# One step later for the attention's sums and the norm's turns in a fused two-block model kernel

## The reference, cut to what matters

```python
def stick_breaking_mixer(xn, k_sh, v_sh, w_q, w_out):
    ...
        z = jnp.einsum('bhqd,bhnsd->bhqns', qi, kb).astype(jnp.float32)
        log_keep = jnp.where(mask, jax.nn.log_sigmoid(-z), 0.0)
        cs_in = jnp.einsum('bhqnj,js->bhqns', log_keep, tri)
        blk = cs_in[..., 0]
        after = lax.cumsum(blk, axis=3, reverse=True) - blk
        a = jnp.where(mask, jnp.exp(z + cs_in + after[..., None]), 0.0)
        outs.append(jnp.einsum('bhqns,bhnsd->bhqd', a.astype(vb.dtype), vb))

def peer_ffn(xn, w_q, subkeys, u, v):
    ...
    def block(args):
        xc, ec, gc = args
        hid = jnp.einsum('cd,ced->ce', xc, jnp.take(u, ec, axis=0)).astype(jnp.float32)
        w = (gc * jax.nn.gelu(hid, approximate=False)).astype(xc.dtype)
        return jnp.einsum('ce,ced->cd', w, jnp.take(v, ec, axis=0))
```

## Time and profile before

| | |
|---|---|
| median of three runs | 2362.85 us (2358.72 to 2370.2) |
| the profiled execution | 2362.11 us, its span in the trace 2360.3 us |
| PE busy | 1934.7 us (82%) |
| DVE busy | 1629.4 us (69%) |
| ACT, POOL busy | 800.8 us, 661.1 us |
| DMA | 746.58 MB, mean 316 GB/s |
| mean granted TensorE clock | 0.905 of full |

### The profile page before, as it was taken

How to read it: one execution, slowest core, us unless ns; L and a number is a source line. 1 busy time by engine, 2 the same in 40 slices (tenths; PEclk the granted TensorE clock), 3 DMA queues, 4 the chain that set the end, 5 groups by cost and what they waited for, 6 DMA issues and landing times. The chain is left out here.

```text
span 2360.3 us, 32786 instructions
## 1 busy us (share of the span) xinstructions
PE 1934.7 (82%) x12376; PEld 1260.4 (53%) x12376; DVE 1629.4 (69%) x3789; ACT 800.8 (34%) x1826; POOL 661.1 (28%) x657
## 2 busy tenths in 40 slices
PE   3999996688686679889869888885878884999798
PEld 3887886665242136546526555651434432767664
DVE  5668876477978677655667798767798544368853
ACT  3112222133342342454343366344323224233222
POOL 2222110044354433343332335434334430000000
PEclk9999998899797789989989999997898996899899
DMA  8998773179999999999999989999899995222200
GB/s 332 370 363 314 258 262 113 40 323 418 369 409 421 421 408 418 419 414 419 409 412 360 409 304 419 419 411 412 334 419 417 419 419 204 94 81 81 98 11 27
DMA packets 124686, 746.58 MB, mean 316 GB/s; under 512 B 13536, under 2 KB 16608, under 8 KB 56304
## 3 DMA queue, kind: packets, MB, share of 16 engines
q0 software_dynamic: 93792, 610.66, 64.2%
q1 hardware_dynamic: 30736, 133.82, 14.7%
HBM read 741.02 MB, written 3.41 MB: 315 GB/s over the span
## 5 line engine op out<-in xcount | busy, mean ns | idle before, releaser
L1947 DVE CUSTOM_DVE_ANT_0 got<-got,xk 128x1024 f32<-128x1024 f32 x512 | 620.5, 1224 | 318.2 <-DMA got<-in_peer_uv,idx 301.5
L1850 POOL DMA_INDIRECT got<-in_peer_uv,idx x512 | 586.1, 1145 | 906.7 <-PE ps L1812 817.0
L1812 PE MATMUL ps<-got,diag 64*64 64x512 f32 x3936 | 580.6, 684 | 191.2 <-ACT diag L1907 137.6
L1902 ACT ACTIVATE gelu<-eye,hid 128x64 f32<-128x64 f32 x492 | 170.5, 347 | 791.8 <-DVE hid L1947 784.5
L1812 PEld LDWEIGHTS ps<-got,diag 64*64 64x64 f32 x3936 | 121.4, 144 | 441.6 <-ACT diag L1907 274.7
L1342 PE MATMUL ps<-xT,ring 128*128 128x256 f32 x928 | 233.4, 399 | 0.0
L1342 PEld LDWEIGHTS ps<-xT,ring 128*128 128x128 f32 x928 | 174.4, 197 | 77.2 <-issue 55.1
L1028 PE MATMUL ps<-xT,ring 128*128 128x256 f32 x768 | 187.6, 393 | 6.1 <-ACT xT L1143 3.8
L1907 ACT ACTIVATE diag<-gelu,gate 128x64 f32<-128x64 f32 x492 | 171.1, 348 | 46.1 <-ACT gelu L1902 1.1
L1028 PEld LDWEIGHTS ps<-xT,ring 128*128 128x128 f32 x768 | 142.2, 193 | 82.3 <-issue 56.2
L192 POOL DMA_DIRECT2D vring<-in_vslabs x136 | 72.3, 532 | 273.4 <-DVE in_b_psums L304 136.9
(11 more groups left out here) (618 smaller groups left out, 2462.5 us busy)
## 6 DMA issues: line engine op xcount, KB each, us to landing
ring<-in_small SPq DMA_DIRECT2D x158, 512.0 KB
vring<-in_vslabs POOLq DMA_DIRECT2D x136, 512.0 KB, 6.9
ring<-in_slabs SPq DMA_DIRECT2D x18, 2048.0 KB, 10.7
got<-in_peer_uv,idx POOLq DMA_INDIRECT x512
h<-in_x SPq DMA_DIRECT2D x2, 2048.0 KB, 7.9
w_out<-in_slabs SPq DMA_DIRECT2D x2, 2048.0 KB, 9.9
out<-h SPq DMA_DIRECT2D x4, 512.0 KB, 2.6
bias_rows<-brow POOLq DMA_DIRECT2D x1, 1280.0 KB, 4.7
```

The source lines that it names most:

```text
L1812: mm = nc.tensor.matmul(ps[to:to + HALF, i, :], diag[own, d % NDIAG, :], got[own, n % GRING, 1, 512 * g:512 * g + 512], start=(k == 0), st ...
L1850: nc.gpsimd.indirect_dma_start(out=got[:, n % GRING].rearrange("p a d -> p (a d)"), out_offset=None, in_=table, in_offset=bass.IndirectOff ...
L1902: nc.scalar.activation(gelu_of[:, n % 2, :], eye2[:], ACT.Gelu, scale=hid[:, w % 2, k:k + 1]).then_inc(gelu_done, 1)
L1947: nc.vector.tensor_tensor_reduce(row_in, row_in, xk[:, w % 2, :], 1.0, 0.0, ALU.mult, ALU.add, hid[:, w % 2, k:k + 1]).then_inc(dotted, 1)
```

## The change

For pass 1 alone, two numbers of the side plan go up by one. The first step of the turns is 5 instead of 4, so the turns and all that follows them stand one step later, while mean, root and scaling keep steps 2 and 3; the plan has 149 steps instead of 148. And "sums" stands at 5 instead of 4 from its head's first step, so its two parts come at 5 and 6, while "top" stays at 4 and "total" at 7. No instruction is added or removed on any engine; buffers, banks and the arithmetic stay as they are. Since `side_pace` works from the plan, its costs and the slot of each step follow.

```diff
@@ side_plan @@
         each, pitch = (1 if p else 2), 6
         asks = [(0, -4, -2)] if p else [(0, -7, -5), (1, -4, -2)]
-        stages = {"product": 0, "take": 2, "soft": 2, "top": 4, "sums": 4, "total": 7, "expo": 8, "output": 9, "return": 11}
+        stages = {"product": 0, "take": 2, "soft": 2, "top": 4, "sums": 5 if p else 4, "total": 7, "expo": 8, "output": 9, "return": 11}
         at = {"mean": 2, "root": 2, "scale": 3}
-        jobs, s = [], 4
+        jobs, s = [], 5 if p else 4
         jobs += [(s + j // 2, "turn", j) for j in range(4)]
```

## The result

The kernel after takes 2370.56 us, median of 18 runs (2366.2 to 2378.97); the kernel before took 2363.22 beside it (18 runs, 2357.34 to 2370.2). The ratio of the times is 1.003, with a 95% interval of 1.002 to 1.0041: slower, by 7.3 us in the medians. The forecast was 2364.5 in a range of 2354 to 2373, and "within 0.5%" at 0.87. The sign and the class hold, the median is in the range; the size is three times the 2.4 us forecast.

A forecast was written before the change was run, and what follows sets the result against it. Pass 1 was taken as bound by DMA transfers save 15 us of idle. DVE 1.2 us late at slot 345 plus 2.4 made 3.6, less 1.2 in hand: +2.4 on 2362.11 gave 2364.5 us, range 2354 to 2373.

The forecast's parts named there:

- Where the steps go, and PE's order: Planner's slots for each step; in heads 3 to 6, 2.9 us of PE work comes between the sums' two parts.
- The norm's turns: Norm and queries: PE's 0.41 us wait filled, a dot product falls behind DVE's wait; DVE enters the attention 0.8 us later.
- Heads 0 to 2: Slots 298 to 313: PE's 13.9 us of waits go, DVE gains 1.6 us, transfers 3 to 5 us ahead at slot 324.
- Head 3: Attention: "total", which waited 2.80 us, costs 2.1 us more; DMA waits of the next dot products hide 1.5.
- Head 4: Attention: "total", which did not wait before, now waits for the sums' second part, +2.3 us.
- Heads 5 and 6: Attention: "total" waits about 1.5 us each, softplus waits of 3.7 us with head 7 go; these nearly cancel.
- Head 7 and its queue: End of attention: last exponential 1.2 + 2.4 = 3.6 us later, 1.2 us in hand, so the DMA is 2.4 us later.
- That lead is spent: The DMA lead from heads 0 to 2 is used up in the ring of 8 buffers, whatever its size.
- (1): Attention: waits shorter or last output's queue covered, DMA stays 3 to 5 us ahead; 2357 to 2359 us, chance 0.31.
- (2): Attention: nothing that counts changes, ring fills as before, DVE sets the pace; 2361 to 2363 us, chance 0.11.
- (3): Heads 3 on: softplus starts as much later as "total" ends, so its waits stay; +11.3 us, 2373 us, chance 0.13.
- The other sign of being wrong: Profile after: a granted clock differing by more than 0.02, which the forecast had not counted.

The follow-up runs named there:

- after again: The kernel after, unchanged, run once more for a second profile; 2364.38 us, slots 263 to 384 in 383.3 us.
- before again: The kernel before, unchanged, run once more for a second profile; 2367.37 us, slots 263 to 384 in 380.6 us.
- e2: The kernel before with only the turns and all behind them one step later, sums ahead of the next product; 2366.95 us, ratio 1.0008.
- e6: The kernel before with sums later for heads 0 to 2 only, head 0's "take" in slot 296, parts ahead of the product; 2363.75 us, 0.9996.
- e9: The kernel after with sums' parts ahead of the next head's product for heads 3 to 6 only; 2363.37 us, ratio 0.9997 to before.
- e3: The kernel after, same slots, but PE does the sums' parts ahead of the next head's product within a step; 2360.22 us, ratio 0.9988 to before.
- e5: The kernel before, every step in its slot, only the sums' second part done behind the next head's product; 2370.35 us, ratio 1.0028.
- e10: The kernel after with sums' parts ahead of the next head's product for heads 0 to 2 only; 2368.32 us, ratio 1.0017 to before.
- e1: The kernel before with only the sums one step later, the turns as before; 2375.54 us, ratio 1.0046.

## Why the prediction was right in kind and short in size

The forecast followed DVE from slot to slot. How much later the dot products start than before, each against its own slot 263, shows where it went short. "Forecast" adds the prediction's terms as they stand: 0.8 - 1.6 + 2.1 - 1.5 up to slot 325, then 2.3 for head 4, then 2 x 1.5 - 3.7 for heads 5 and 6; that gives 1.4 at slot 345, where the prediction says 1.2.

| us later at the dot product of slot | 325 | 329 | 335 | 341 | 345 | 353 |
|---|---|---|---|---|---|---|
| forecast | -0.2 | 2.1 | | | 1.4 | |
| after against before | -0.6 | 4.4 | 6.9 | 6.7 | 5.2 | 6.8 |
| after again against before again | -1.4 | 3.3 | 5.6 | 5.1 | 3.6 | 5.0 |

- **Where the steps go, and PE's order**: right, as the rows of slots 326 and 327 show. (A slip in the reading of the earlier trace rows, on which nothing rests: the DMA is full from slice 9 on, slice 8 has 0.7.)
- **The norm's turns**: the start of slot 293 was forecast 0.8 us later in all and came 0.1 us earlier, against slot 263 (in after again 0.7 us later than before). The first turns of the queries are taken ahead of the dot product of slot 292, as forecast. e2 agrees that the turns cost little: 1.0008, not told from 1.
- **Heads 0 to 2**: PE's 13.9 us of waits for "top" went, as forecast. 9.0 us came back as waits for the diagonals, which I had not named: PE now stands where a dot product hasn't been made, since DVE is the slow engine there (48.16 of 50 us busy). Gather 318 was forecast for about 1398.5; it was issued at 1401.97, less the 3.4 us 1398.6. The DMA's lead, 3 to 5 us forecast at slot 324, was 2.5 MB at slot 320; at 419 GB/s that is 6.0 us, less the 2.7 us that slot 320 came later: 3.3 us. That this lead is worth nothing at the end of the pass was the boldest step, and e6 bears it out.
- **Head 3**: "total" waits 4.83 us instead of 2.80, 2.0 more, where I had 2.1. The match is luck. In this trace PE made the first part and the weighted sum behind it at a granted clock of 0.64 (1416.60 to 1421.30 us, the levels being 0.50 and 1.00). In after again the same work ran at 1.00 and "total" waited 3.21 us, 0.5 more than the 2.75 of before again. In e9 the clock was 0.50 there (1417 to 1421 us), and "total" waited 4.6 us in spite of the old order. The first parts, after and after again:

```profile
1417.61 1.61 PE L1099 MATMUL ps<-sb_sp,const 128*128 128x128 f32 x4
```

```profile
1415.26 0.92 PE L1099 MATMUL ps<-sb_sp,const 128*128 128x128 f32 x4
```

Nor did this wait cost DVE anything: the kernel before waited 1.25 and 1.26 us for transfers at the dot products of slots 322 and 323, the kernel after did not, and at slot 325 it was 0.6 us ahead. I had let these waits hide 1.5 us. Gather 325 waited 4.99 us on POOL, but less the 3.4 us it was issued at 1424.2, and before at 1424.30. So the first new dip is the end of the lead (gather 322 was still issued 4.2 us earlier), not yet a loss.
- **Head 4**: this is the term that was mis-sized most. "+2.3 us" was 5.0 us. "Total" waited 3.24 us, and ahead of it the add L1954 of slot 326 waited 2.74 us for ACT, where a like wait before had 0.98. The forecast priced only what PE puts in front of "total". On ACT four copies (L1881) come first; they stand behind the dot products of slots 320 to 322, which came late by head 3's "total", and began at 1430.13 - 3.4, 1.1 us later than before (1425.61). The exponential, the softplus and the add's `hid` follow them on ACT. So DVE had made up for head 3 and ACT had not. The second pair of traces has 3.01 us for "total" and 2.52 against 0.48 us for the add.
- **Heads 5 and 6**: the second step that failed. I wrote: "For heads 5 and 6 it waits about 1.5 us each, but 'top' is a slot later and no longer waits for the softplus, 3.7 us in three waits with head 7. These nearly cancel." The waits of "total" were 2.70 and 1.16 us, and the waits of "top" did go. Head 6 did cancel (6.9 to 6.7 us in the table) and head 7's "top" gave 1.5 us back. Head 5 did not: it cost 2.5 us, since ACT's chain starts at "total" and was late with it, and the lateness reached DVE through the next thing that stands behind softplus on ACT, the add's `hid` (2.08 us). From slot 329 to 345 this is +0.8 us, where the terms give -0.7.
- **Head 7 and its queue**: the output product came 9.3 us later, not 3.6. Of these 5.2 were there at slot 345, 2.4 are the dot product and the add that "total" moved past, as forecast, and 1.6 are a wait of "total" for the second part, which the forecast left out. The dip near 1500 us is there (0.77), and gather 353 with it; of 9.3 us the faster product took 1.6 off, and the pass ends 7.3 later. "That lead is spent", "nothing gives it back": both held, slots 353 to 384 took 99.9 us after 99.4.
- **The rivals**: (1), the lead kept, is excluded by the interval. (2) too: something that counts did happen. (3) had +11.3 us, about as far from the 7.3 as the forecast's 2.4. Its premise, a softplus as late as "total", was half right: it holds in head 5, but DVE met it at the add, not at L1240, where it waited only once, in head 3. So PE's order and DVE's waits were the forecast's, ACT's lateness was the rival's, and the size lay between the two. The other sign of being wrong, a granted clock more than 0.02 away, did not show in the whole (0.906 against 0.905), but did in slots 320 to 353 (0.89 against 0.92). That it is not the cause can be seen in before again: it has 0.88 there and took 88.1 us, after again 0.89 and 90.8 us.
- **What is shown, and what argued**: that PE's order carries the loss is shown by taking it out, e3 (0.9988) and e9 (0.9997). e5 (1.0028) shows that the order alone can cost as much in the slots of before, there mostly in heads 0 to 3. That the loss of this change lies in heads 3 to 6 follows from e9; e10 is the weaker half, since the two intervals overlap a little. How the 7.3 us divide between the heads rests on single traces, good to 2.5 us, of which the second pair has the same order of sizes. e1's 1.0046 is above the change's 1.003, but their intervals overlap. And e3 can't be told from the kernel before, so no version here is shown to beat it.

## What to carry over

When a step is moved by one in a plan that several engines follow, look first at what it comes to stand behind on its own in-order engine in the new place: here 1.78 us of product between two halves of a sum cost more than the right slot won. A stall that seems to cancel against another has to be followed through each engine that starts from it, since a late engine hands its lateness on in whatever it does next. And idle transfers won early in a pass may be worth nothing at its end: here a ring of 8 buffers had spent the lead within a few slots, and e6, which won them alone, took 0.9996 of the time before.

## What was not expected of the hardware

A full DMA share was not one rate. The stretches before (1430 to 1500 us) and after differ by 4% at shares of 1.01 and 1.00: 420 and 403 GB/s, the latter in a stretch where POOL's gathers come late. e3 has 417. Both kernels also have 405 GB/s in 1250 to 1340 us, at 1.00 and 1.01. The share is the packets' own time, so packets that take longer do not show in it. A thin queue may be the cause in the kernel after; no run tried it. In 1250 to 1340 us the mix differs too: SP's loads have 23% of the packet time there and some 6% in 1430 to 1500 us. The mix can't be all of it, since 1500 to 1530 us before has 25% and 418 GB/s.

```profile
1430.00:1500.00 70.00, 57.74 (x299) 37.92 (x296) 62.85 (x93) 44.92 (x89) 37.77 (x27) 0.91 1.01 420
```

The clock can halve the speed of the work behind a wait. After PE's wait of 5.03 us for the copy L1881, 16 matrix products of a weighted sum took 3.69 us at a granted clock of 0.50, and 16 of the same shape 1.95 us at 1.00, after 8 us of work in which the clock rose (both in the kernel after):

```profile
1432.60:1436.20 3.60, 3.60 (x16) 0.79 (x16) 3.53 (x5) 3.48 (x5) 2.03 (x2) 0.50 1.04 419
...
1440.82:1442.69 1.87, 1.87 (x17) 0.51 (x16) 1.77 (x5) 0.79 (x4) 0.48 (x1) 1.00 0.88 364
```

That is 1.2 GHz instead of 2.4. The wait before was 3.85 us and the same work took 2.65 us. The last output product went the other way, 3.35 us before at 0.50 and 1.78 after at 1.00, behind waits of nearly the same length (3.74 and 3.45 us); no run shows why. The Trainium skill, "TensorE: Matmul & The Clock Gate", Part 1, says that an idle TensorE falls to the lower rate; the first case agrees, and the last shows that the length of one wait doesn't settle it.

The table load on ACT took 1.28 us, and the next activation started 0.02 us behind it (1458.00 to 1459.30). The Trainium skill, "ScalarE: Activation LUTs", What ACT_TABLE_LOAD costs, gives about 1.28 us for the load and 1.38 us more for a drain. The first figure agrees. For the second there is no room in these rows, on either side of the load: the activation ahead of it ends at 1457.99. The measurement decides.
